# The first norm fed straight from PSUM, and an output product normed by blocks of tokens: one change to a three-block kernel

## What is computed

```python
def rms_norm(x, w):
    xf = x.astype(jnp.float32)
    y = xf * lax.rsqrt(jnp.mean(xf * xf, axis=-1, keepdims=True) + NORM_EPS)
    return (y * w.astype(jnp.float32)).astype(x.dtype)

def hybrid_layer(x, ...):
    ...
    x = x + rms_norm_2(merged @ w_out, norm_g[1])
    h = rms_norm_2(x, norm_g[2])
    gt, up = jnp.split(h @ w_ffn_in, 2, axis=-1)
    x = x + rms_norm_2((jax.nn.silu(gt) * up) @ w_ffn_out, norm_g[3])
    return x
```

## Time and profile before

| | us |
|---|---|
| median of 3 runs (lowest, highest) | 3339.97 (3339.40, 3340.59) |
| the profiled execution | 3339.14 |
| its span | 3337.4 |
| TensorE busy | 3283.3 (98%) |
| VectorE, ScalarE, GpSimd busy | 1191.9, 1234.2, 1381.5 |
| mean granted TensorE clock | 0.994 |

### The profile page before, as it was taken

How to read it: one execution, slowest core, us unless ns; L and a number is a source line. 1 busy time by engine, 2 the same in 40 slices (tenths; PEclk the granted TensorE clock), 3 DMA queues, 4 the chain that set the end, 5 groups by cost and what they waited for, 6 DMA issues and landing times.

```text
span 3337.4 us, 41197 instructions
## 1 busy us (share of the span) xinstructions
PE 3283.3 (98%) x16823; PEld 2688.7 (81%) x16823; DVE 1191.9 (36%) x2070; ACT 1234.2 (37%) x1864; POOL 1381.5 (41%) x614
## 2 busy tenths in 40 slices
PE   8999999999999999999999999999999999999998
PEld 6888888888888888888888887778866796868887
DVE  4220476332203220376332205743454334442211
ACT  4332435432314232445443214521355452443222
POOL 5444532454445444532354445553211242434443
PEclk9999999999999999999999999999999999999999
DMA  5332321233333332321233333238233432323332
GB/s 136 97 100 95 89 70 51 76 95 95 95 101 95 95 97 99 90 70 52 71 94 98 98 96 100 76 91 185 72 85 91 136 84 55 95 71 93 98 105 70
DMA packets 465432, 305.52 MB, mean 92 GB/s; under 512 B 68024, under 2 KB 437032, under 8 KB 465244
## 3 DMA queue, kind: packets, MB, share of 16 engines
q1 hardware_dynamic: 464424, 302.84, 32.2%
q10 hardware_dynamic: 820, 0.04, 0.0%
HBM read 296.20 MB, written 6.64 MB: 91 GB/s over the span
## 4 chain that ended last, share of the span: by engine, by line
PE 88%; DVE 7%; ACT 1%; DVEq 1%; issue 1%; DMA 1%; SPq 0%; POOL 0%; ACTq 0%
PE ps L528 37%; PE ps L546 14%; PE ps L3082 5%; PE ps L1247 4%; PE ps L899 3%; PE ps L2759 3%; PE ps L2404 3%; PE ps L1239 2%; PE ps L1454 2%; PE ps L1335 2%; DVE h_lo L388 2%; PE ps L3060 1%; PE ps L2083 1%; PE ps L2771 1%; PE ps L2803 1%; PE ps L2781 1%
## 5 line engine op out<-in xcount | busy, mean ns | idle before, releaser
L179 POOL TENSOR_TENSOR w_lo<-w_raw,w_hi 128x1024 fp32r<-128x1024 f32 x518 | 1278.3, 2470 | 1911.5 <-ACT w_hi L171 1910.7
L171 ACT ACTIVATE w_hi<-w_raw 128x1024 fp32r<-128x1024 f32 x518 | 544.0, 1054 | 1010.1 <-PE ps L546 365.9
L528 PE MATMUL ps<-h_hi,w_hi 128*128 128x512 f32 x1952 | 770.5, 395 | 4.1 <-DVE h_lo L388 3.8
L528 PE MATMUL ps<-h_hi,w_lo 128*128 128x512 f32 x1952 | 759.9, 389 | 0.0
L528 PE MATMUL ps<-h_lo,w_hi 128*128 128x512 f32 x1952 | 759.8, 389 | 0.0
L528 PEld LDWEIGHTS ps<-h_hi,w_hi 128*128 128x128 f32 x1952 | 366.6, 188 | 91.7 <-DVE h_lo L388 11.9
L528 PEld LDWEIGHTS ps<-h_lo,w_hi 128*128 128x128 f32 x1952 | 366.7, 188 | 79.4 <-issue 4.6
L528 PEld LDWEIGHTS ps<-h_hi,w_lo 128*128 128x128 f32 x1952 | 366.6, 188 | 76.4
L546 PE MATMUL ps<-a_hi,w_hi 128*128 128x512 f32 x640 | 249.0, 389 | 0.0
L546 PE MATMUL ps<-a_lo,w_hi 128*128 128x512 f32 x640 | 249.0, 389 | 0.0
L546 PE MATMUL ps<-a_hi,w_lo 128*128 128x512 f32 x640 | 249.0, 389 | 0.0
(11 more groups left out here) (505 smaller groups left out, 5305.5 us busy)
## 6 DMA issues: line engine op xcount, KB each, us to landing
w_raw<-in_w_in_dram SPq DMA_DIRECT2D x128, 512.0 KB, 3.9
w_raw<-in_ffn_w_gate_dram SPq DMA_DIRECT2D x88, 512.0 KB, 3.8
w_raw<-in_ffn_w_up_dram SPq DMA_DIRECT2D x88, 512.0 KB, 3.8
w_raw<-in_ffn_w_down_dram SPq DMA_DIRECT2D x88, 512.0 KB, 3.4
w_raw<-in_w_ffn_in_dram SPq DMA_DIRECT2D x44, 512.0 KB, 3.8
w_raw<-in_w_out_dram SPq DMA_DIRECT2D x24, 512.0 KB, 3.5
w_raw<-in_w_ffn_out_dram SPq DMA_DIRECT2D x22, 512.0 KB, 3.6
w_raw<-in_w_branch_dram SPq DMA_DIRECT2D x16, 512.0 KB, 4.2
```

The lines of the kernel that those rows point to most:

```text
L171: act.activation(self.hi[:, s, :, :], self.raw[:, s, :, :], ACT.Copy).then_inc(self.halved[s], 1)
L179: pool.tensor_tensor(self.lo[:, s, :, :], self.raw[:, s, :, :], self.hi[:, s, :, :].bitcast(F32), ALU.subtract)\
L528: mm = pe.matmul(out, w, (c.h_hi, c.h_lo)[low][:, k, :], start=(k == 0 and i == 0), stop=(k == KD - 1 and i == 2))
```

## The change

**Front.** Chunk 0 is as before. For chunks 1 to 7 `h_hi` (ScalarE) and `h_lo` (VectorE) are computed from the PSUM bank directly. The copies to `x_T` are split: VectorE makes 0, 2, 4, 6, 7, ScalarE makes 1, 3, 5, each once VectorE's `h_lo` of that chunk is out. The squares come only when all chunks are in `x_T`, the additions are VectorE's, and TensorE makes one sum with ones, behind the first gate and the first up tile (`late_sum`). `w_hi` of tile 1 stands behind h_hi 5 (it stood behind h_hi 4), that of tile 2 ahead of the squares.

**Output product.** Tokens by features: bank b holds half b % 2 of the features for 128 tokens b // 2. As soon as a pair of banks is closed, ScalarE squares both into one column each and takes the root; VectorE takes the reciprocal and scales both banks by it and by the gain row (loaded once, 128 x 1024) into `mixed`; TensorE turns the result back into the same banks, four transposes a bank, and VectorE adds them to `x_T`. The transposes of pair 0 stand behind bank 3 of the product, those of pair 1 behind bank 5, the others at the end. Then eight `h_hi`, eight `h_lo`, `w_hi` of tile 2, and squares and additions as in the front, with the sum behind two tiles.

```diff
@@ load_x, ScalarE
             for m in range(KD):
-                act.wait_ge(c.x_done.sem, xb + m + 1)
-                act.activation(c.h_hi[:, m, :], c.x_T[:, m, :], ACT.Copy, scale=c.gains[:, g, m:m + 1]).then_inc(c.h_high.sem, 1)
-                if m == 4:
+                if m == 0:
+                    act.wait_ge(c.x_done.sem, xb + 1)
+                else:
+                    act.wait_ge(c.closed.sem, cb + m + 1)
+                act.activation(c.h_hi[:, m, :], c.ps[:, bank[m], :] if m else c.x_T[:, m, :], ACT.Copy, scale=c.gains[:, g, m:m + 1])\
+                    .then_inc(c.h_high.sem, 1)
+                if m in (2, 4, 6):
+                    act.wait_ge(c.h_low.sem, lb + m)
+                    act.activation(c.x_T[:, m - 1, :], c.ps[:, bank[m - 1], :], ACT.Copy).then_inc(c.x_done.sem, 1)
+                if m == 5:
                     c.w.high_to(act, 1)
+            c.w.high_to(act, 2)
+            act.wait_ge(c.x_done.sem, xb + KD)
+            for m in range(KD):
                 if m >= 3:
-                    act.wait_ge(c.added.sem, ab + m - 1)
+                    act.wait_ge(c.added.sem, ab + m - 2)
                 act.activation(acc[:, :] if m == 0 else sq[:, m % 2, :], c.x_T[:, m, :], ACT.Square).then_inc(c.squared.sem, 1)
@@ load_x, VectorE
+            dve.wait_ge(c.closed.sem, cb + 1)
+            copy(0)
+            h_rest(c, dve, g, 0)
+            for m in range(1, KD):
+                dve.wait_ge(c.h_high.sem, c.h_high.n + m + 1)
+                if m == KD - 1:
+                    copy(m)
+                low(m)
+                if m in (2, 4, 6):
+                    copy(m)
+            for m in range(1, KD):
+                dve.wait_ge(c.squared.sem, qb + m + 1)
+                dve.drain()
+                dve.tensor_tensor(acc[:, :], acc[:, :], sq[:, m % 2, :], ALU.add).then_inc(c.added.sem, 1)
@@ ffn, TensorE
-                w.used_by(column_product(c, pe, t0 + 2 * i, c.ps[:, p, :], i == 0, square_on if i == 0 else None), t0 + 2 * i)
-                if i == 0 and square_on is None:
+                w.used_by(column_product(c, pe, t0 + 2 * i, c.ps[:, p, :], i == 0), t0 + 2 * i)
+                if i == 0 and not late_sum:
                     sum_on(pe)
                 if i >= 2:
                     pe.wait_ge(c.up_out.sem, ub + i - 1)
                 w.used_by(column_product(c, pe, t0 + 2 * i + 1, c.ps[:, 2 + p, :]), t0 + 2 * i + 1)
+                if i == 0 and late_sum:
+                    sum_on(pe)
@@ post_norm, SP
+        w.load_to(sp, t0 + SLOTS)
+        sp.dma_start(gain[:, :], bass.AP(tensor=g_post.tensor, offset=g_post.offset, ap=[[0, P], [1, D]]))\
+            .then_inc(c.gain_row_loaded.sem, 16)
         w.load_to(sp, t0 + n + SLOTS - 1)
@@ post_norm, TensorE
+        def turn(t):
+            for b in (2 * t, 2 * t + 1):
+                pe.wait_ge(c.inverted.sem, ib + b + 1)
+                for k in range(4):
+                    mm = pe.transpose(ps[:, b, k * P:(k + 1) * P], blocks[:, b, k * P:(k + 1) * P], c.ident[:, :])
+                mm.then_inc(c.turned.sem, 1)
...
+        for b in range(2 * TT):
+            for j in (n - 2, n - 1):
+                mm = product(j, b, False, j == n - 1)
...
+            if b in (3, 5, 7):
+                turn(b // 2 - 1)
+        turn(TT - 1)
@@ post_norm, ScalarE
+        for b in range(2 * TT):
+            t = b // 2
+            bank_done(act, b)
+            act.activation(sq[:, b % 2, :], ps[:, b, :], ACT.Square, scale=D ** -0.5, accum_out=part[:, b:b + 1])\
+                .then_inc(c.squared.sem, 1)
+            if b % 2:
+                act.drain()
+                act.wait_ge(c.summed.sem, mb + t + 1)
+                act.activation(c.rcol[:, t:t + 1], part[:, b:b + 1], ACT.Sqrt, bias=part[:, 8 + t:9 + t])\
+                    .then_inc(c.rooted.sem, 1)
         for m in range(KD):
+            act.wait_ge(c.x_done.sem, xb + KD - 1 + m // 4)
+            act.activation(c.h_hi[:, m, :], c.x_T[:, m, :], ACT.Copy, scale=c.gains[:, g, m:m + 1]).then_inc(c.h_high.sem, 1)
+        w.high_to(act, t0 + n + 2)
@@ post_norm, VectorE
+        for t in range(TT):
+            dve.wait_ge(c.squared.sem, qb + 2 * t + 1)
+            dve.tensor_scalar(part[:, 8 + t:9 + t], part[:, 2 * t:2 * t + 1], EPS, None, ALU.add).then_inc(c.summed.sem, 1)
+            if t:
+                add(2 * t - 2)
+                add(2 * t - 1)
+            dve.wait_ge(c.rooted.sem, rb + t + 1)
+            dve.reciprocal(c.rcol[:, t:t + 1], c.rcol[:, t:t + 1])
+            dve.drain()
+            for b in (2 * t, 2 * t + 1):
+                half = b % 2
+                dve.scalar_tensor_tensor(blocks[:, b, :], ps[:, b, :], c.rcol[:, t:t + 1], gain[:, 512 * half:512 * half + 512],
+                                         ALU.mult, ALU.mult).then_inc(c.inverted.sem, 1)
+        add(2 * TT - 2)
+        add(2 * TT - 1)
+        for m in range(KD):
+            h_rest(c, dve, g, m)
```

More of the change, by code:

```diff
@@ L494, in _, with copy, low @@
             dve.drain().then_inc(c.gain_loaded.sem, 1)
-            for m in range(KD):
-                dve.wait_ge(c.closed.sem, cb + m + 1)
+            def copy(m):
                 dve.tensor_copy(c.x_T[:, m, :], c.ps[:, bank[m], :]).then_inc(c.x_done.sem, 1)
[L498 to L510, removed]
+            def low(m):
+                dve.scalar_tensor_tensor(out=c.h_lo[:, m, :], in0=c.ps[:, bank[m], :], scalar=c.gains[:, g, m:m + 1],
+                                         in1=c.h_hi[:, m, :].bitcast(F32), op0=ALU.mult, op1=ALU.subtract).then_inc(c.h_low.sem, 1)
+            dve.wait_ge(c.closed.sem, cb + 1)
[12 more added lines that the diff above has]
+                dve.tensor_tensor(acc[:, :], acc[:, :], sq[:, m % 2, :], ALU.add).then_inc(c.added.sem, 1)
         c.closed.n += KD
@@ L747, in post_norm @@
     sq, acc = scratch
-    rows_product(c, t0, n, hi, lo, ready, order, free)
-    qb, ab, nb = c.squared.n, c.added.n, c.summed.n
-    c.rooted.n += 1
-    c.inverted.n += 1
-    c.summed.n += 2
+    gain = nc.alloc_sbuf_tensor_at("gain_row_mixed", [P, D], F32, offset=c.sel_at)
+    part = c.rstd
+    ps = c.ps
+    cb, qb, rb, ib, tb, xb, mb, ab = (x.n for x in (c.closed, c.squared, c.rooted, c.inverted, c.turned, c.x_done, c.summed, c.added))
+    c.gain_row_loaded.n += 16
+    c.closed.n += KD - 1
@@ new lines, in _, with product @@
+    @c.on.tensor
+    def _(pe):
+        def product(j, b, first, last):
+            t, half = b // 2, b % 2
+            s = (t0 + j) % SLOTS
+            for i, (x, weight) in enumerate(((hi, w.hi), (lo, w.hi), (hi, w.lo))):
+                mm = pe.matmul(ps[:, b, :], x[:, j, t * P:(t + 1) * P],
+                               weight[:, s, 4 * half:4 * half + 4, :].rearrange("p k f -> p (k f)"),
+                               start=first and i == 0, stop=last and i == 2)
+            return mm
+        def turn(t):
[4 more added lines that the diff above has]
+                mm.then_inc(c.turned.sem, 1)
+        for j in range(n - 2):
+            w.ready(pe, t0 + j)
+            ready(pe, j)
+            for b in (order if j == 0 else range(2 * TT)):
+                if j == 0:
+                    free(pe, b)
+                mm = product(j, b, j == 0, False)
+            w.used_by(mm, t0 + j)
+        for j in (n - 2, n - 1):
+            w.ready(pe, t0 + j)
+            ready(pe, j)
+        for b in range(2 * TT):
+            for j in (n - 2, n - 1):
+                mm = product(j, b, False, j == n - 1)
+                if b == KD - 1:
+                    w.used_by(mm, t0 + j)
+            if b < KD - 1:
+                mm.then_inc(c.closed.sem, 1)
+            if b in (3, 5, 7):
+                turn(b // 2 - 1)
+        turn(TT - 1)
@@ L771, in _ @@
-    @c.on.gpsimd
-    def _(pool):
-        w.low_to(pool, t0 + n + 1)
-    c.closed.n += KD - 1
-    c.squared.n += KD
-    c.added.n += KD - 1
-    spread = c.ps[:, 6, :]
-    @c.on.tensor
-    def _(pe):
-        pe.wait_ge(c.added.sem, ab + KD - 1)
-        for t in range(TT):
-            mm = pe.matmul(c.ps[:, 7, t:t + 1], acc[:, t * P:(t + 1) * P], c.ones[:, 0:1], start=True, stop=True)
-        mm.then_inc(c.summed.sem, 1)
-        pe.wait_ge(c.inverted.sem, c.inverted.n)
-        pe.matmul(spread, c.ones[:, :], acc[:, :], start=True, stop=True).then_inc(c.summed.sem, 1)
@@ L790, in _, with add @@
[L790 to L793 removed]
+            act.activation(acc[:, :] if m == 0 else sq[:, m % 2, :], c.x_T[:, m, :], ACT.Square).then_inc(c.squared.sem, 1)
     @c.on.vector
     def _(dve):
+        def add(b):
+            t, half = b // 2, b % 2
+            dve.wait_ge(c.turned.sem, tb + b + 1)
+            x = c.x_T[:, 4 * half:4 * half + 4, t * P:(t + 1) * P]
+            dve.tensor_tensor(x, x, ps[:, b, :].rearrange("p (k q) -> p k q", q=P), ALU.add).then_inc(c.x_done.sem, 1)
@@ L820, in _ @@
[L820 to L831 removed]
+    c.squared.n += KD
+    c.rooted.n += TT
+    c.inverted.n += 2 * TT
```

74 lines of the change are left out of this document (24 added, 50 removed).

## The result

| | before | after |
|---|---|---|
| median, us (lowest to highest, runs) | 3339.54 (3336.61 to 3340.59, 7) | 3328.33 (3325.38 to 3329.00, 7) |
| the profiled execution, us | 3339.14 | 3328.33 |
| its span, us | 3337.4 | 3326.6 |
| mean granted TensorE clock | 0.994 | 0.994 |

The ratio is 0.9967 [0.9957, 0.9977]: faster by 0.33%. A second measurement of the same kernel gave 3328.86 (3328.52 to 3330.11, 6 runs), ratio 0.9972 [0.9960, 0.9983].

What follows compares the result with a forecast made beforehand. TensorE was taken as the bound (88% of the chain), so time changes only where it is held up. Savings of 3.45 + 8.8 = 12.25, rounded to 12, from 3339.14 gave 3327.1; plus 0.83 for the median, 3328.0 us, range 3325.0 to 3332.0.

Steps and rivals of the forecast that it cites:

- The output product's term: Behind the output product: second gate tile starts earlier than 2975.55; 9.1 us saved, 8.8 after the clock; bounds 6.5 to 10.3.
- the 0.3 for the clock: Output product: low clock for 3 to 4 us delays the gate tile 1.6 us, mostly hidden; 0.3 us taken off.
- wait of 1.15 us: Sum behind the output product: TensorE was to wait 1.15 us for VectorE's additions, given as a sign.
- Turn 0: Output product, transposes of the first pair of banks: cost 1.2 us, with a wait of 0.8 us.
- The front's term: Front: second gate tile starts at 31.8 instead of 35.27, 3.45 us saved; bounds 2 to 4.35.
- the cover of 0.6: Front: w_lo of tile 4 done at 42.1, wanted by TensorE at 42.7, so in time by 0.6 us.
- (d): Late sum makes w_lo of tile 4 late in one or both places; loss of 1 to 2 us, 3329.5; chance 0.09.
- (a): The forecast itself for the whole kernel, own range 3326.5 to 3329.8 us; chance 0.50.
- (b): Both places: thinner covers, with dear turns, low clock and dearer PSUM reads; saves 8.5 us, 3331.5; chance 0.17.
- (c): Both places: the lock doesn't catch the first addition; saves 14.6 us, 3325.4; chance 0.12.
- (e): Additions of turned blocks dearer, or blocks run one after another behind the product; saves 4 to 6.5 us, 3334.5; chance 0.09.
- (f): Slower: transposes and gaps at the output product set off a long low clock; 3348 us at 40 us; chance 0.03.

Runs made afterwards that it cites:

- e6: After plus seven unused 512-column TensorE products ahead of the output product's last transposes and seven behind, against after: 3328.05 us, ratio to before 0.9969.
- e5: After with the bias rows on VectorE moved to the sixth pair of tiles of the first FFN, against after: 3328.50 us, ratio to before 0.9972.
- e4: After with squares 1 to 7 written to two free PSUM banks in both places, against after: 3327.78 us, ratio to before 0.9966.

## Why the prediction held, step by step

**The time.** 3328.0 was forecast and 3328.33 measured, but two errors cancel. From the profiled execution the sum gave 3327.1, and that execution took 3328.33: 1.2 us too little. The 0.83 us by which the median stood above the profiled execution was then added, and in after there is no such difference. That the forecast came within 0.4 us is luck: it is in effect the median of three runs of before, 3339.97, less 12. The 59 runs of before beside the experiments have a mean of 3338.8, 1.2 us lower, and the gain between the means of before and after is 10.2 us, 1.8 less than the 12.

**The output product's term (8.8 forecast, 8.7 measured)** holds in its parts. In this list forecasts are less the 2.2 us by which after was ahead at the second mark. Turn 2 at 2945.3 (2945.33 measured); last transposes ending at some 2949.5 (eight transposes from 2948.20, 1.31 long); h_lo from 2950.5 (2950.37); TensorE's first chunk at 2951.3 (2951.27); acc ready at 2963.35 (2963.32); second gate tile, with the 0.3 for the clock, at 2964.55. Its second matmul stands at 2964.84, so it began at 2964.6. The clock fell as the bound assumed and cost the two tiles 1.5 us (the sum was reached at 2963.75, forecast 2962.2), and as the forecast said most of it was hidden by acc. One stated sign was wrong in consequence: the second sum shows no wait of 1.15 us. It appears, as 0.9, when the clock is kept up (e6). Turn 0 cost 1.07 for 1.2, turn 1 0.79 (2941.72 to 2942.51) for 0.9. Turn 0 was to wait 0.8 us, which is wrong too: its transposes took 1.31 where those of turn 1 took 1.03, so its wait was 0.3. The 8.7 itself is one execution's; the product alone, with a longer low clock, has 7.3.

**The front's term (3.45 forecast, 2.5 measured at the first mark)** is right up to the second gate tile (31.8 forecast, 31.83 measured; the sum waits 0.69 for 0.85) and fails at one step: the bias rows were to be "blocked by w_lo of tile 3 to 33.8. Reciprocal 33.9", and of w_lo of tile 4 I said "It holds with 0.6 us." I had the lock catch the last of the three lines, as in the earlier trace rows. Here w_lo of tile 3 starts at 30.93, when VectorE is in the sixteen copies. One of them lasted 2.39 us where the median of the sixteen is 0.155:

```profile
L1063 DVE COPY f<-tab x16: 150/155/2387, 30.8 to 34.1; 48x3 f32<-48x3 f32 x3, 48x4 f32<-48x4 f32 x2, 48x6 f32<-48x6 f32 x2, 48x10 f32<-48x10 f32 x2
```

The rest of the rows stand behind it, so the reciprocal came 1.25 us late and used up the cover of 0.6. So what the prediction gave as a sign of being wrong, "if TensorE waits for w_lo of tile 4", came true at the front. It is the effect of rival (d), a little under its price of 1 to 2 us, but not by the cause that (d) names: in e5 the sum is as late as in after and the wait is gone. Behind the rule is an assumption that I stated too narrowly: "a VectorE operation with two SBUF operands waits until w_lo is over". The copies read one operand from SBUF and wait as well. The Trainium skill has both halves: in "SBUF — State Buffer", section SBUF: two separate sides, the lock is also taken by a VectorE operation in a two-port performance mode, which a copy from SBUF to SBUF in fp32 triggers. I had used the one half alone; the row above and e4's 3.63 us agree with the other.

**The PSUM operand** did what the prediction took from the earlier trace rows: seven h_lo from PSUM at 735 to 751 ns, no dearer than the fastest from SBUF (736 ns), and none held. Only two of the seven tell of the lock, those that start at 21.09 and 22.96, since w_lo ran beside them from 20.56 to 22.95 and from 23.15. The dearer price by the errata table of "VectorE: DVE Perf Modes" in the Trainium skill, weighed in the prediction, doesn't show in these rows. e4 adds the causal side: seven additions with an operand in PSUM are 1.1 to 1.2 us shorter, in both places.

**Does the front pay at all?** In the profiled executions it does: its part of the stream is 2.5 us or more shorter in each of them that has it (first mark 261.2 or less, against 263.7 to 264.3), and the two executions of the front alone end 1.3 to 3.1 us ahead of the two of before (spans 3334.6 and 3334.3 against 3337.4 and 3335.9). In the timed runs it is worth nothing alone (21 runs, mean 3338.8; before, 59 runs, mean 3338.8) and 1.5 us on top of the product part (13 runs of after, mean 3328.6, against 3330.1). Worked out from the spread of these runs, the standard error of the first difference is 0.5 us and that of the second 0.8: a gain of 2.5 us alone would have shown, and the 1.5 is not clear of noise. Every run also lists its mean granted clock. Time multiplied by it is roughly what the run would take at 2.4 GHz throughout, since TensorE is busy for 98% of the span:

| means | us | clock | us times clock |
|---|---|---|---|
| before (59 runs) | 3338.8 | 0.99322 | 3316.2 |
| front alone (21) | 3338.8 | 0.99267 | 3314.3 |
| product alone (7) | 3330.1 | 0.99371 | 3309.2 |
| after (13) | 3328.6 | 0.99369 | 3307.6 |

By this measure the front alone is 1.9 us shorter and gives this back to a lower clock somewhere in the span, and 1.9 + 7.0 = 8.9 agrees with the 8.6 of both. But the clock is listed to 0.001, 3.3 us each, and the two sets of after differ by as much (0.99414 and 0.99317). The spread of time times clock within a kernel is about 1.6 us, so the standard error of the 1.9 is 0.4, and the 1.9 is clear of zero, if the runs are independent. Whether the front's edit lowers the clock later on, or the sets only fell so, stays open; no profiled execution of it shows the gain given back. What is shown: of the measured 10 to 11 us most is the output product's, 7.3 to 8.7 by the marks and 8.9 by the times of the product alone. The front's share of the time is not shown.

**Rivals.** (a) happened, with the effect of (d) at the front. (b), thinner covers at the turns, didn't: they were cheaper than forecast. (c) was refuted in both places: seven additions took 6.48 and 6.60, and 5.37 where they can't be held. (e) was refuted by the timeline; the blocks are scaled within the product. (f) didn't occur: the granted clock was back at 0.88 in the slice at 2954.

## What to carry to other kernels

Where VectorE and GpSimd share a stretch, give each VectorE operation on the path one operand in PSUM, if a bank is free: here it cost nothing and removed the hold of each operation so treated (h_lo 0 and the bias rows, which have none there, are still held). A chain of per-chunk norms between two products is worth reshaping so that its scalings lie within the first product (7.3 to 8.7 us here by the marks), and the sum over features put behind two tiles belongs to it (5 us of wait otherwise). When work is moved earlier on a busy engine, the small instructions queued behind it, here sixteen copies of 0.15 us, must be placed against the lock anew.
